# A complex state recurrence rewritten in a rotating frame, with the order of the convolution's taps changed

## The chip, the cores and the metric

One core of a Trainium2 chip runs the whole kernel. The metric is device microseconds (us) of one execution. Engines are named as in the profile: PE is TensorE (matmuls; PEld its weight loads), DVE VectorE, ACT ScalarE, POOL GpSimd, SP the engine that issues most DMAs.

## What is computed

Two layers of a hybrid block over 128 context tokens and 128 latent tokens (the two sequences are s = 0 and 1, NS = 2), width 1024, all in float32. One input projection feeds three branches: a convolution of width 31 over 512 channels, a bidirectional diagonal complex state space (S5, 32 groups of 16 channels, 64 complex states each) and attention with 8 query and 2 key heads. Gates, a merge and an output projection follow. The part of the reference that the change concerns:

```python
def _ssm_combine(e1, e2):
    a1, b1 = e1
    a2, b2 = e2
    return a1 * a2, a2 * b1 + b2
...
        lam_bar = jnp.exp(lam * dt)
        b_bar = ((lam_bar - 1.0) / lam)[..., None] * lax.complex(b_re[dirn], b_im[dirn])
        bu = jnp.einsum('blgc,gpc->blgp', uc, b_bar)
        if not want_final:
            bu = bu.at[:, edge].add(lam_bar * h0)
        a = jnp.broadcast_to(lam_bar, bu.shape)
        _, hs = lax.associative_scan(_ssm_combine, (a, bu), axis=1, reverse=rev)
        if want_final:
            fin = hs[:, 0] if rev else hs[:, -1]
        y = y + jnp.einsum('blgp,gcp->blgc', hs, c_mat).real
```

## The kernel before

Every engine runs one list of stages, written by hand in `order(l)` (one call for each layer), and does of each stage its own part, in the order of the list; semaphores join them. Weights come through SP as slabs of 512 KB into a ring of four (`raw`). For the early projections (`cg`, `ssm`, `ca`) and the late ones, ScalarE (L1086) and VectorE (L1358) split each weight chunk into a high and a low part and TensorE multiplies three times (L1032 to L1034); `q`, `kv`, `sg`, `gg` and `ag` are plain float32 (L756).

The state space works on chunks of L = 4 tokens, so 32 chunks (NCHUNK) and 32 steps. The partitions hold 64 forward and 64 backward states. The stages around the change, in the list's order:

- `tab` (L1466 on): VectorE and ScalarE make the powers of lambda and tables of them, from small parameters; GpSimd computes from them and B the matrices `pre` (`preP`), which TensorE transposes to E (`preE`). The tables of layer 1 are made in layer 0, after `att` 0.
- `xn`: ScalarE squares and sums x, GpSimd makes the rsqrt (L1783, L1779), VectorE scales x into `xn`, which lies in H (L1529). TensorE transposes it (`hT`).
- `pack`, `UT`: the tokens' inputs go through DMA and a ScalarE copy (L1229) into groups, TensorE transposes them, ScalarE and VectorE copy them to Uz (L1567).
- `S`: TensorE multiplies E by Uz (L867), eight banks; ScalarE copies the forward half to H, VectorE the backward half (L1575).
- `cp`: GpSimd computes CP, the powers times C (L1779, tiles tA, tB and EC), in 18 instructions, once the last bank of S is filled. `K` (TensorE, L880) needs CP, and the Toeplitz blocks M (`toeplitz`, 20 small DMAs) need K.
- `scan`: 32 steps of four VectorE instructions of 128 elements (`scan_step`, L1391). In steps 16 to 31 a tap of the convolution (`conv_tap`, L1423, 128x256) follows each; 31 taps for each of the tiles 0 and 1. The tiles 2 and 3 have their taps in `att` 1 and later.
- `qkn`: norms and rotary of q and k on VectorE, with a rsqrt on GpSimd, and a wait for it, for each sequence.
- `Y`: ScalarE and VectorE copy quarters of H to HY (L1296, L1676), TensorE multiplies (L961, L963), ScalarE copies out. Then `qkT` (transposes of q and k; VectorE copies to kz, L1630), `att` 0, and `gelu` (VectorE adds, ScalarE, L1312), whose result TensorE transposes in `geT` (L765) before `att` 1.

VectorE helpers: `tt_` is L1358, so that line has nearly all of its tensor_tensors; `needs` and `makes` put waits only on what an instruction reads.

```python
                    for c in range(c0, c1):
                        for i in range(4):
                            scan_step(l, c, i)
                            if taps_left:
                                conv_tap(*taps_left.pop(0))
```

## Time and profile before

| | |
|---|---|
| three runs | 846.63, 848.39, 848.56 us |
| median | 848.39 us |
| span of the profiled execution, from the first to the last instruction | 845.0 us |
| its own time | not given apart from the span |
| PE busy | 712.7 us, 84% |
| DVE busy | 605.8 us, 72% |
| ACT busy | 316.0 us, 37% |
| POOL busy | 172.6 us, 20% |
| mean granted TensorE clock | 0.936 |
| chain that ended last | PE 52%, DVE 36%, ACT 3%, DMA 3% |

A timeline row has start, duration, engine, line, operation, out<-in, shapes and count; in brackets stands the idle time of the engine before it and what ended it. Where a row counts several instructions, the duration is that of all. A row of a stretch has, after its length, the busy time and count of each engine, then the clock granted to TensorE as a share of full speed (1.00 is 2.4 GHz, its other level is 1.2 GHz), the DMA engines' share and GB/s. On the chain shares say who ended last, not what is slow: an engine may stand in it for work that another delayed.

### The profile page before, as it was taken

How to read it: one execution, taken by the hardware profiler on the slowest of the kernel's cores; microseconds unless marked ns; L12 is line 12 of the kernel's file. 1: busy time of each engine (PE TensorE's matmuls, PEld its weight loads, DVE VectorE, ACT ScalarE, POOL GpSimd, SP SyncE). 2: the span in 40 equal slices, each digit the busy share in tenths (PEclk: the TensorE clock that was granted, in tenths of full speed). 3: DMA queues.
4: the chain of work that ended last, by engine and by line, in shares of the span. 5: the costliest groups of instructions: out<-in, count | busy, mean ns of one | idle time of the engine just before them, and what ended most of it. 6: DMA issues, size and time to landing. Idle time of an engine off the chain costs nothing.

```text
span 845.0 us, 9392 instructions
## 1 busy us (share of the span) xinstructions
PE 712.7 (84%) x3294; PEld 469.8 (56%) x3294; DVE 605.8 (72%) x1103; ACT 316.0 (37%) x563; POOL 172.6 (20%) x121
## 2 busy tenths in 40 slices
PE   4957899990779994988999999999907698999996
PEld 1145665550721533776778558655507456787785
DVE  3378689997355589768866554899973568888664
ACT  1244451111323322454655355401213433545552
POOL 1067449202000009033000100492020000000000
PEclk9979999995789997999999999999967698999999
DMA  6864335350067471554565475454220034555661
GB/s 208 282 146 118 125 128 173 110 145 28 3 155 232 141 239 61 150 150 146 154 184 168 147 236 165 137 166 118 73 99 1 26 99 124 176 174 155 195 177 55
DMA packets 79339, 117.64 MB, mean 139 GB/s; under 512 B 27437, under 2 KB 31869, under 8 KB 79293
## 3 DMA queue, kind: packets, MB, share of 16 engines
q1 hardware_dynamic: 78460, 116.52, 45.6%
q10 hardware_dynamic: 832, 0.53, 0.3%
q8 instruction: 26, 0.43, 0.2%
q14 instruction: 21, 0.16, 0.1%
HBM read 112.51 MB, written 1.38 MB: 135 GB/s over the span
## 4 chain that ended last, share of the span: by engine, by line
PE 52%; DVE 36%; ACT 3%; DMA 3%; issue 2%; SPq 2%; POOL 1%; DVEq 0%; ACTq 0%; POOLq 0%
PE proj L1032 11%; PE proj L1034 10%; PE proj L1033 10%; DVE H L1358 8%; PE proj L730 8%; DVE cvacc L1423 7%; DVE qkt L1358 7%; PE side L765 4%; PE proj L756 3%; DVE qM_split L1358 3%; PE side L963 2%; DVE wide_split L1358 2%; DMA raw<-in_w_ada 2%; DVE H L1575 2%; DVE gates_split L1358 2%
## 5 line engine op out<-in xcount | busy, mean ns | idle before, releaser
L756 PE MATMUL proj<-raw,hT 128*128 128x512 f32 (+1 forms) x320 | 125.1, 551 | 0.0
L1423 DVE SCALAR_TENSOR_TENSOR cvacc<-cvpad,taps,cvacc 128x256 f32<-128x256 f32 x240 | 123.1, 541 | 0.0
L1358 DVE TENSOR_TENSOR wide_split<-raw,wide_split 128x512 fp32r<-128x512 f32 x118 | 90.6, 773 | 41.4 <-ACT wide_split L1086 40.3
L1086 ACT ACTIVATE wide_split<-raw 128x512 fp32r<-128x512 f32 x118 | 74.4, 632 | 95.9 <-PE proj L1034 95.9
L756 PEld LDWEIGHTS proj<-raw,hT 128*128 128x128 f32 x320 | 60.3, 190 | 60.4 <-issue 58.4
L730 PE MATMUL proj<-raw,cond 128*2 128x512 f32 x192 | 88.8, 617 | 5.9 <-DMA raw<-in_w_ada 5.9
L1358 DVE TENSOR_TENSOR H<-H,qkt 128x128 f32<-128x128 f32 x128 | 75.5, 590 | 1.2
L1032 PE MATMUL proj<-wide_split,H_split 128*128 128x512 f32 x154 | 65.0, 422 | 13.2 <-DVE wide_split L1358 12.7
L1783 POOL TENSOR_SCALAR st<-st 128x1 f32<-128x1 f32 (+1 forms) x12 | 3.9, 324 | 336.9 <-DVE st L1692 148.7
L961 PE MATMUL side<-qM,Uz 128*64 128x64 f32 x128 | 20.5, 248 | 54.3 <-DVE HY L1676 54.3
L1033 PE MATMUL proj<-wide_split,H_split 128*128 128x512 f32 x154 | 62.8, 408 | 0.0
L1034 PE MATMUL proj<-wide_split,H_split 128*128 128x512 f32 x154 | 62.7, 407 | 0.0
L1358 DVE TENSOR_TENSOR utok_split<-raw,utok_split 128x512 fp32r<-128x512 f32 x58 | 45.4, 783 | 16.9 <-ACT utok_split L1086 16.0
L730 PEld LDWEIGHTS proj<-raw,cond 128*2 128x2 f32 x192 | 15.6, 87 | 71.0 <-issue 56.1
L1358 DVE TENSOR_TENSOR qM_split<-raw,qM_split 128x512 fp32r<-128x512 f32 x32 | 38.6, 1218 | 20.3 <-ACT qM_split L1086 20.3
L1086 ACT ACTIVATE utok_split<-raw 128x512 fp32r<-128x512 f32 x58 | 36.6, 632 | 41.3 <-PE proj L1034 41.3
L961 PEld LDWEIGHTS side<-qM,Uz 128*64 128x64 f32 x128 | 15.0, 162 | 55.9 <-issue 55.9
L1032 PEld LDWEIGHTS proj<-wide_split,H_split 128*128 128x128 f32 x154 | 29.9, 194 | 26.4 <-DVE wide_split L1358 18.6
L1032 PE MATMUL proj<-qM_split,mixed_split 128*128 128x512 f32 x64 | 27.4, 428 | 13.6 <-DVE qM_split L1358 13.6
L1358 DVE TENSOR_TENSOR qkt<-H,lamI 128x128 f32<-128x128 f32 x64 | 37.3, 583 | 1.4
L1196 ACT ACTIVATE gates<-proj 128x512 f32<-128x512 f32 x12 | 7.1, 597 | 75.9 <-PE proj L756 62.6
L1779 POOL TENSOR_TENSOR tA<-cT,lamr 128x1024 f32<-128x1024 f32 (+1 forms) x12 | 19.7, 1640 | 74.5 <-PE side L867 73.7
(235 smaller groups left out, 1491.1 us busy)
## 6 DMA issues: line engine op xcount, KB each, us to landing
raw<-in_w_in SPq DMA_DIRECT2D x104, 512.0 KB, 3.8
raw<-in_w_ada SPq DMA_DIRECT2D x48, 512.0 KB, 4.5
raw<-in_w_out SPq DMA_DIRECT2D x16, 512.0 KB, 4.2
raw<-in_w_ssm_glu SPq DMA_DIRECT2D x8, 512.0 KB, 5.2
raw<-in_w_ssm_out SPq DMA_DIRECT2D x8, 512.0 KB, 3.8
raw<-in_w_attn_out SPq DMA_DIRECT2D x8, 512.0 KB, 4.1
raw<-in_w_conv_out SPq DMA_DIRECT2D x8, 512.0 KB, 3.9
raw<-in_w_in SPq DMA_DIRECT2D x8, 256.0 KB, 2.8
```

Of the source, the lines that this page charges most:

```text
L730: m = T.matmul(proj.bank(stg + (b,))[0:NS, :], cond[:, :, kt], w[:, 0, W * b:W * b + W], start=(kt == 0), stop=(kt == DT - 1))
L756: m = T.matmul(proj.bank((l, u, s))[:, 0:n], lhs[:, s, kt, :], w[:, i, :], start=(kt == 0), stop=last)
L765: return T.transpose(out, in_, ident[0:k, 0:k])
L961: T.matmul(o, Uz[:, g, :], M[:, :, g // 2, :], start=True, stop=False)
L963: m = T.matmul(o, HY[:, q % 2, gi, r, :, :].rearrange("p s k -> p (s k)"), CP[:, r, 1:L + 1, g, :], start=False, stop=(r == 1))
L1032: T.matmul(bank[:, :], hi, whi, start=(kt == 0), stop=False)
L1033: T.matmul(bank[:, :], hi, wlo, start=False, stop=False)
L1034: m = T.matmul(bank[:, :], lo, whi, start=False, stop=last)
L1086: S.activation(chunk_parts(m)[0], chunk_raw(m), ACT.Copy).then_inc(chunk_hi, 1)
L1358: return V.tensor_tensor(out, a, b, op)
L1423: m = V.scalar_tensor_tensor(acc, src, taps[:, t, j:j + 1], acc, ALU.mult, ALU.add)
L1779: return Q.tensor_tensor(out, a, b, op)
```

## The change

The recurrence h(k+1) = lambda h(k) + b(k), with complex lambda, is written for h turned back by the angle of lambda times k. There the factor is the real decay, the same for real and imaginary part, and a quarter of the groups (8 of 32; 1024 elements in a lane) is done by one scan instruction (tensor_tensor_scan, listed as SCALAR_TENSOR_TENSOR of H from decay and H). VectorE turns b by a table `spin` of cosines and sines, scans, and turns back in place; Y reads H directly, so HY's copies go. GpSimd makes `spin` by doubling (5 rounds of 4 instructions) from lambda's angle. H has a new layout, with the chunks innermost. ScalarE now copies both halves of S. The taps of tiles 0 and 1 stand in three blocks of 14, 24 and 24: before `UT`, behind `qkn`, and behind `tab` and `spin` (in layer 1 behind `att` 0). `convT` moves ahead of `pack`. The tables lamR, lamI and the tile h0 go; the scratch for DMA rings is smaller, and the semaphores follow.

```diff
 def order(l):
...
-            + [("unit", "ssm"), ("unit", "ca"), ("pack",)] + ([("preE", 0, 1)] if l == 0 else [])
-            + [("bz", 0), ("UT",), ("S",), ("cp",), ("convT", 0), ("convT", 1), ("scan", 0, 16, ()),
-               ("unit", "q"), ("unit", "kv"), ("scan", 16, NCHUNK, (0, 1)),
-               ("unit", "sg"), ("K", 0), ("bz", 1), ("qkn", 0), ("qkn", 1)]
+            + [("unit", "ssm"), ("unit", "ca"), ("convT", 0), ("convT", 1), ("pack",)]
+            + ([("preE", 0, 1)] if l == 0 else [])
+            + [("bz", 0), ("conv", 0, 7, (0, 1), None), ("UT",), ("S",), ("cp",), ("unit", "q"), ("unit", "kv")]
+            + [("states", i) for i in range(4)]
+            + [("unit", "sg"), ("K", 0), ("bz", 1), ("qkn", 0), ("qkn", 1), ("conv", 7, 19, (0, 1), None)]
             + [("unit", "gg"), ("K", 1), ("unit", "ag"), ("Y",), ("qkT", 0), ("qkT", 1), ("att", 0)]
-            + nxt("small", n) + nxt("tab", n) + nxt("ada", n, 0) + nxt("adaT", n, 0)
+            + nxt("small", n) + nxt("tab", n) + nxt("spin", n) + [("conv", 19, TAPS, (0, 1), None)]
+            + nxt("ada", n, 0) + nxt("adaT", n, 0)
...
 def stages():
-    out = [(0, s) for s in (("cond",), ("small", 0), ("tab", 0), ("taps", 0), ("ada", 0, 0), ("xn", 0, 0), ("xn", 0, 1),
+    out = [(0, s) for s in (("cond",), ("small", 0), ("tab", 0), ("spin", 0), ("taps", 0), ("ada", 0, 0), ("xn", 0, 0), ("xn", 0, 1),
...
-        H, Hs = shared("H", [P, NCHUNK + 1, ROW])
+        H, Hs = shared("H", [P, G, 2, NS, NCHUNK])
...
 TensorE, stage Y
-                        pe.wait_ge(hy_fwd, 4 * l + q + 1)
-                        pe.wait_ge(hy_bwd, 4 * l + q + 1)
+                        pe.wait_ge(states_done, 4 * l + q + 1)
...
-                                m = T.matmul(o, HY[:, q % 2, gi, r, :, :].rearrange("p s k -> p (s k)"),
+                                m = T.matmul(o, H[:, g, r, :, :].rearrange("p s k -> p (s k)"),
...
 ScalarE, stage S
-                        dst = H[0:64, 1:NCHUNK + 1, 16 * i:16 * i + 16].rearrange("p k x -> p x k")
-                        S.activation(dst, side.bank(key)[0:64, :].rearrange("p (x k) -> p x k", k=NCHUNK),
-                                     ACT.Copy).then_inc(side.freed(key), 1)
+                        src = side.bank(key)[:, :].rearrange("p (x k) -> p x k", k=NCHUNK)
+                        dst = H[:, 4 * i:4 * i + 4, :, :, :].rearrange("p g r s k -> p (g r s) k")
+                        S.activation(dst[0:64], src[0:64], ACT.Copy).then_inc(side.freed(key), 1)
+                        S.activation(dst[64:128, :, ::-1], src[64:128], ACT.Copy).then_inc(side.freed(key), 1)
...
 VectorE
-            def scan_step(l, c, i):
...
+            def states(l, q):
+                g0 = GQ * q
+                here = H[:, g0:g0 + GQ, :, :, :]
+                lanes = lambda t: t.rearrange("p g r s k -> p g (r s) k")
+                for i in (2 * q, 2 * q + 1):
+                    side.drained(dve, ("S", l, i))
+                if q == 0:
+                    side.filled(dve, ("E", l, 7))
+                    dve.wait_ge(zeroed, N_ZERO)
+                    dve.wait_ge(tab_done, l + 1)
+                    dve.wait_ge(spin_done, l + 1)
+                def turn(k0):
+                    for i in range(2):
+                        by = spin[:, i, g0:g0 + GQ, k0:k0 + NCHUNK].unsqueeze(2).to_broadcast([P, GQ, 2 * NS, NCHUNK])
+                        makes(("turned", i), tt_(lanes(turned[i]), lanes(here), by))
+                if q:
+                    dve.wait_ge(states_done, 4 * l + q)
+                turn(1)
+                makes("decay", V.tensor_copy(decay[:, :, :, 1:NCHUNK], ss[:, 14, g0:g0 + GQ].unsqueeze(2).unsqueeze(3)
+                                             .to_broadcast([P, GQ, 2 * NS, NCHUNK - 1])))
+                needs(("turned", 0), ("turned", 1))
+                for r, op in ((0, ALU.add), (1, ALU.subtract)):
+                    tt_(here[:, :, r, :, 1:NCHUNK], turned[0][:, :, r, :, 0:NCHUNK - 1],
+                        turned[1][:, :, 1 - r, :, 0:NCHUNK - 1], op)
+                    tt_(ends[:, 0, r, g0:g0 + GQ], turned[0][:, :, r, 0, NCHUNK - 1], turned[1][:, :, 1 - r, 0, NCHUNK - 1], op)
+                V.memset(here[:, :, :, 0, 0], 0.0)
+                makes("here", V.tensor_copy(here[:, :, :, 1, 0], t5[:, 3:5, g0:g0 + GQ].rearrange("p r g -> p g r")))
+                needs("here", "decay")
+                flat = here.rearrange("p g r s k -> p (g r s k)")
+                makes("here", V.tensor_tensor_scan(flat, decay[:, :, :, :].rearrange("p g x k -> p (g x k)"), flat, 0.0,
+                                                   ALU.mult, ALU.add))
+                needs("here")
...
+                turn(0)
...
+                needs(("turned", 0), ("turned", 1))
+                for half in range(2):
+                    rows_ = slice(64 * half, 64 * half + 64)
+                    for r, op in ((0, ALU.subtract), (1, ALU.add)):
+                        dst = here[rows_, :, r, :, :]
+                        if half:
+                            dst = dst[:, :, :, ::-1]
+                        m = tt_(dst, turned[0][rows_, :, r, :, :], turned[1][rows_, :, 1 - r, :, :], op)
+                m.then_inc(states_done, 1)
...
 GpSimd
+                elif k == "spin":
+                    ll = stg[1]
+                    pool.wait_ge(tab_done, ll + 1)
+                    for w in (1, 2, 4, 8, 16):
+                        n = 2 * G * w
+                        t1, t2 = (t[:, 0:n].rearrange("p (r g k) -> p r g k", r=2, g=G) for t in (tB, bzf))
+                        known = spin[:, :, :, 1:w + 1]
+                        by = [spin[:, r:r + 1, :, w:w + 1].to_broadcast([P, 2, G, w]) for r in range(2)]
+                        link(tt_(t1, known, by[0]))
+                        link(tt_(t2, known, by[1]))
+                        link(tt_(spin[:, 0, :, w + 1:2 * w + 1], t1[:, 0], t2[:, 1], ALU.subtract))
+                        m = tt_(spin[:, 1, :, w + 1:2 * w + 1], t1[:, 1], t2[:, 0], ALU.add)
...
```

How the instructions stand, at three places. First VectorE in layer 0, from the end of the early projections to the recurrence; `mixed` is the convolution's input, Uz the state space's input by groups. Before:

```order
L1546 SCALAR_TENSOR_TENSOR mixed<-th,proj 128x512 x2
L1567 COPY Uz<-side 64x8x64 x2
L1575 COPY H<-side 64x16x32 x8
L1583 COPY H<-h 128x128
L1358 TENSOR_TENSOR qkt<-H,lamI 128x128
L1358 TENSOR_TENSOR qkt<-H,lamR 128x128
L1358 TENSOR_TENSOR H<-H,qkt 128x128 x2
```

And with the change, behind the same row of `mixed`:

```order
L1452 TENSOR_SCALAR cvacc<-cvpad,taps 128x256 x2
L1455 SCALAR_TENSOR_TENSOR cvacc<-cvpad,taps,cvacc 128x256 x12
L1596 COPY Uz<-side 64x8x64 x2
L1351 TENSOR_TENSOR pre<-H,spin 128x1024 x2
L1405 COPY decay<-ss 128x32x31
L1351 TENSOR_TENSOR H<-pre 128x8x2x31
L1351 TENSOR_TENSOR ends<-pre 128x8
L1351 TENSOR_TENSOR H<-pre 128x8x2x31
L1351 TENSOR_TENSOR ends<-pre 128x8
L1412 MEMSET H 128x16
L1413 COPY H<-t 128x16
L1416 SCALAR_TENSOR_TENSOR H<-decay,H 128x1024
```

Fourteen taps (cvacc) now stand ahead of Uz, and in place of eight copies and the first of 32 steps the rows show the first half of one quarter of four.

Second GpSimd at the start, from the spread of the time steps to the rsqrt of x (the rows with st). Before:

```order
L1790 MEMSET st 128x12
L1796 COPY a<-ldt 32x128
L1783 ISA
L1783 TENSOR_SCALAR st<-st 128x1
L1779 TENSOR_TENSOR st<-st 128x1
```

And with the change, from the third round of the doubling on:

```order
L1776 TENSOR_TENSOR tB<-spin 128x256
L1776 TENSOR_TENSOR bz<-spin 128x256
L1776 TENSOR_TENSOR spin<-tB,bz 128x32x4 x2
L1776 TENSOR_TENSOR tB<-spin 128x512
L1776 TENSOR_TENSOR bz<-spin 128x512
L1776 TENSOR_TENSOR spin<-tB,bz 128x32x8 x2
L1776 TENSOR_TENSOR tB<-spin 128x1024
L1776 TENSOR_TENSOR bz<-spin 128x1024
L1776 TENSOR_TENSOR spin<-tB,bz 128x32x16 x2
L1780 TENSOR_SCALAR st<-st 128x1
L1776 TENSOR_TENSOR st<-st 128x1
```

The first two rounds, on 128x64 and 128x128, stand ahead of these. The rsqrt, the last two rows, now comes behind twenty instructions on `spin`.

Third VectorE in layer 0 behind `att` 0, from the end of `tab` for layer 1 to the bias and skip of Y (`utok`, `mixed`), whose sum the GELU takes. Before:

```order
L1515 COPY lamR<-lamr 128x128
L1519 TENSOR_SCALAR lamI<-lami 128x32x2
L1520 COPY lamI<-lami 128x32x2
L1522 MEMSET h 128x128
L1524 COPY h<-t 128x32
L1525 COPY h<-t 128x32
L1358 TENSOR_TENSOR ada<-side,modc 128x16
L1358 TENSOR_TENSOR utok<-utok,rows 128x512
L1358 TENSOR_TENSOR mixed<-mixed,utok 128x512
L1358 TENSOR_TENSOR utok<-utok,rows 128x512
L1358 TENSOR_TENSOR mixed<-mixed,utok 128x512
L1358 TENSOR_TENSOR ada<-side,modc 128x16
```

And with the change:

```order
L1351 TENSOR_TENSOR ss<-ss 128x32 x2
L1547 COPY ss<-tB 128x32
L1351 TENSOR_TENSOR ss<-bz 128x32 x2
L1351 TENSOR_TENSOR ss<-ss 128x32
L1552 TENSOR_SCALAR ss<-ss 128x32
L1351 TENSOR_TENSOR spin<-bz,ss 128x32 x2
L1455 SCALAR_TENSOR_TENSOR cvacc<-cvpad,taps,cvacc 128x256 x24
L1351 TENSOR_TENSOR ada<-side,modc 128x16
L1351 TENSOR_TENSOR utok<-utok,rows 128x512
L1351 TENSOR_TENSOR mixed<-mixed,utok 128x512
L1351 TENSOR_TENSOR utok<-utok,rows 128x512
L1351 TENSOR_TENSOR mixed<-mixed,utok 128x512
```

24 taps now stand between the table and the sum that the GELU waits for.

## Rows read from the trace of the kernel before

**Rows 1.** Busy time by stretch; the first line names the columns.
```profile
core 0: us, PE busy (x) PEld busy (x) DVE busy (x) ACT busy (x) POOL busy (x), PEclk, DMA share, GB/s
117.20:151.70 34.50, 34.50 (x99) 18.09 (x97) 33.93 (x30) 5.18 (x11) 31.66 (x18) 1.00 0.45 138
188.70:215.90 27.20, 0.03 (x2) 0.04 (x1) 21.95 (x54) 4.78 (x4) 4.36 (x4) 0.60 0.09 27
612.00:639.10 27.10, 0.00 (x0) 0.00 (x0) 21.85 (x54) 4.37 (x3) 4.36 (x4) 0.60 0.24 79
```

**Rows 2.** Timeline of PE: S and K in layer 0, geT, S in layer 1.
```profile
109.02 7.38 PE L867 MATMUL side<-Uz,EC 128*128 128x128 f32 x64 [1.01 <-DVE Uz L1567]
...
151.68 4.63 PE L880 MATMUL side<-EC,bz 128*48 128x80 f32 x64
...
275.55 1.09 PE L765 MATMUL side<-ident,mixed 128*128 128x128 f32 x8
...
532.29 7.38 PE L867 MATMUL side<-Uz,EC 128*128 128x128 f32 x64 [1.02 <-DVE Uz L1567]
```

**Rows 3.** Timeline of DVE and ACT: from qkn to the GELU, layer 0, then layer 1.
```profile
200.00 0.82 DVE L1358 TENSOR_TENSOR qkt<-qk 128x640 f32<-128x640 f32 x1
...
214.72 1.97 DVE L1676 COPY HY<-H 64x1024 f32<-64x1024 f32 x2
...
230.75 0.29 DVE L1630 COPY kz<-side 64x128 f32<-64x128 f32 x1 [5.57 <-PE side L765]
...
267.02 0.63 ACT L1312 ACTIVATE mixed<-mixed 128x512 f32<-128x512 f32 x1 [5.20 <-DVE mixed L1358]
...
654.00 0.29 DVE L1630 COPY kz<-side 64x128 f32<-64x128 f32 x1 [5.56 <-PE side L765]
...
668.29 0.63 ACT L1312 ACTIVATE mixed<-mixed 128x512 f32<-128x512 f32 x1 [3.61 <-DVE mixed L1358]
```

**Rows 4.** Timeline of DVE, one step alone, and of POOL in cp.
```profile
152.81 0.29 DVE L1358 TENSOR_TENSOR qkt<-H,lamI 128x128 f32<-128x128 f32 x1
...
153.87 0.29 DVE L1358 TENSOR_TENSOR qkt<-H,lamI 128x128 f32<-128x128 f32 x1
...
116.49 1.93 POOL L1779 TENSOR_TENSOR tA<-cT,lamr 128x1024 f32<-128x1024 f32 x1 [21.20 <-PE side L867]
...
120.52 2.47 POOL L1779 TENSOR_TENSOR EC<-tA,tB 128x1024 f32<-128x1024 f32 x1
...
148.80 1.39 POOL L1779 TENSOR_TENSOR EC<-tA,tB 128x512 f32<-128x512 f32 x1
```

**Rows 5.** Timeline of POOL and DVE in preP, layer 0.
```profile
86.57 2.36 POOL L1779 TENSOR_TENSOR tB<-lami,bbar 128x1024 f32<-128x1024 f32 x1
...
86.97 2.52 DVE L1358 TENSOR_TENSOR gates_split<-raw,gates_split 128x512 fp32r<-128x512 f32 x1
```

**Rows 6.** Timeline of DVE and ACT just before S, layer 0.
```profile
104.44 1.38 DVE L1546 SCALAR_TENSOR_TENSOR mixed<-th,proj 128x512 f32<-128x512 f32 x2 [2.06 <-PE proj L1034]
...
107.62 1.30 DVE L1567 COPY Uz<-side 64x512 f32<-64x512 f32 x2 [1.80 <-PE side L765]
...
101.56 1.90 ACT L1229 ACTIVATE HY<-wide 64x2048 f32<-64x2048 f32 x1
...
107.61 1.07 ACT L1237 ACTIVATE Uz<-side 64x512 f32<-64x512 f32 x2
```

**Rows 7.** Timeline of DVE with no POOL beside it: wide passes and taps.
```profile
304.93 2.36 DVE L1358 TENSOR_TENSOR H_split<-hT,H_split 128x1024 fp32r<-128x1024 f32 x2
307.21 8.80 DVE L1423 SCALAR_TENSOR_TENSOR cvacc<-cvpad,taps,cvacc 128x256 f32<-128x256 f32 x22
```

**Rows 8.** Timeline of POOL, DVE and PE at the start, around xn.
```profile
30.13 0.24 POOL L1783 TENSOR_SCALAR st<-st 128x1 f32<-128x1 f32 x1 [18.88 <-ACT H L1145]
...
32.33 0.75 DVE L1529 TENSOR_SCALAR H<-x,st 128x1024 f32<-128x1024 f32 x1 [0.43 <-POOL st L1779]
...
45.98 1.62 PE L765 MATMUL side<-ident,H 128*128 128x128 f32 x12
```

More of the change, by code:

```diff
@@ L62 @@
 GP = G // 2
-ROW = G * 2 * NS
+GQ = G // 4
 EPS = 1e-6
@@ L290, in build @@
         tt += [bzf[:, 352 * i:352 * i + 352] for i in range(4)]
-        lamR = sb("lamR", [P, ROW])
-        lamI = sb("lamI", [P, ROW])
+        spin = sb("spin", [P, 2, G, NCHUNK + 1])
+        ends = sb("ends", [P, 3, 2, G])
         a32 = sb("a32", [P, 5, P])
@@ L349, in build @@
         nmx = sb("nmx", [P, NS, HEADS, 2])
-        scan_t = qkt[:, 0:2 * ROW].rearrange("p (a b) -> p a b", a=2)
+        decay = sb("decay", [P, GQ, 2 * NS, NCHUNK])
+        turned = [pre[:, i, :, :, :].rearrange("p g j c -> p (g j c)").rearrange("p (g r s k) -> p g r s k", g=GQ, r=2, s=NS)
+                  for i in range(2)]
         ldt = sb("ldt", [P, 2])
@@ L468, in build @@
         ln_pre = sem("ln_pre")
-        N_ZERO = 4
+        N_ZERO = 7
         tab_dt = sem("tab_dt")
@@ L967, in _ @@
                     side.claim(pe, key)
+                    pe.wait_ge(ends_done, l + 1)
                     for r in range(2):
-                        src = H[:, NCHUNK, :].rearrange("p (g r s) -> p r s g", g=G, r=2)[:, r, 0, :]
-                        m = transpose(side.bank(key)[0:G, P * r:P * r + P], src)
+                        m = transpose(side.bank(key)[0:G, P * r:P * r + P], ends[:, 0, r, :])
                     m.then_inc(side.full, 1)
@@ L1631, in _ @@
                 elif k == "conv":
-                    end = 0 if stg[3] is None else chunk_at[(l, "br" + stg[3], WT - 1)] + 1
+                    end = 0 if stg[4] is None else chunk_at[(l, "br" + stg[4], WT - 1)] + 1
+                    if stg[1] == 0:
+                        conv_ready(l)
                     for j in range(stg[1], stg[2]):
-                        for t in (2, 3):
+                        for t in stg[3]:
                             conv_tap(t, j)
@@ L1789, in _ @@
             Q.memset(kz[1][:, :, :], 0.0).then_inc(zeroed, 1)
+            Q.memset(decay[:, :, :, 0], 0.0).then_inc(zeroed, 1)
+            Q.memset(spin[:, 0, :, 0], 1.0).then_inc(zeroed, 1)
+            Q.memset(spin[:, 1, :, 0], 0.0).then_inc(zeroed, 1)
             link(Q.memset(st[:, 128:140], -0.5))
@@ L1797, in _ @@
                                   ldt[0:G, :].unsqueeze(2).to_broadcast([G, 2, SP])).then_inc(ldt_spread, 1)
+                elif k == "spin":
[10 more added lines that the diff above has]
+                        m = tt_(spin[:, 1, :, w + 1:2 * w + 1], t1[:, 1], t2[:, 0], ALU.add)
+                        if w < 16:
+                            link(m)
+                        else:
+                            m.then_inc(spin_done, 1)
+                            pool.wait_ge(spin_done, ll + 1)
                 elif k == "preP":
```

136 lines of the change are left out of this document (43 added, 93 removed).

## The prediction, made before the changed kernel had run

> **What bounds the kernel now.** I read the busy time by stretch first [rows 1]. TensorE works in nearly all of the stretch from 117 to 152 us. From 188.7 to 215.9 us it does almost nothing (0.03 of 27.2 us), and in layer 1 from 612.0 to 639.1 us nothing (27.1 us). VectorE has 22 us of work in each. So twice 27 us is the most that a shorter recurrence could give at these places.
>
> The timelines say what the wait is made of. Call S the start of the matmuls that fill the recurrence's input, 109.02 us in layer 0 and 532.29 in layer 1 [rows 2]; I count from it. VectorE copies, scans 32 steps, normalises q and k from 200.00 to 214.72 (14.7 us, with two waits for GpSimd), and only then makes the copies that Y needs [rows 3]. The first copy of kz, with which attention starts, comes at 230.75, that is S + 121.7; in layer 1 at 654.00, again S + 121.7.
>
> The scan is not long because of its own instructions. A step that runs alone takes 153.87 - 152.81 = 1.06 us. But from 116.49 to 150.19 GpSimd computes CP in 18 tensor_tensor instructions [rows 4], and in the 34.5 us of [rows 1] VectorE gets only 30 instructions through, between seven and eight steps: about 26 us are lost. With wider instructions the exchange is the same: GpSimd's 128x1024 instruction in [rows 5] takes 2.36 us where it takes 1.93 beside short ones [rows 4], and VectorE's 128x512 subtraction takes 2.52 where one of that width takes 0.69 alone (1.38 for two, [rows 6]). One of VectorE's passes gets in for each of GpSimd's, and their times add up.
>
> **The recurrence, costed.** A quarter has two rotations of two 128x1024 products, the decay table, two pairs of an add with 496 elements and a tiny one, small fills, the scan instruction, and four 64x512 adds. Two 128x1024 passes take 2.36 us [rows 7], about 1.14 from start to start. So: rotations 4 x 1.14 = 4.6. Decay 0.6 (a 128x1024 single-input instruction took 0.75 [rows 8]; a 1x copy would be 1.1). 496- and 512-wide adds at half of the 1024's price and a little overhead, 6 x 0.6 = 3.6. Small ones and their waits 0.9. The scan instruction is in no row. Its lower end is one 128x1024 pass, 1.2 us. Its upper end is a quarter of today's steps, 32 x 1.06 / 4 = 8.5 us. I take 1.2, since the operand shapes are those of that pass. Sum 10.9 a quarter, 43.6 a layer. That replaces 32 steps (some 30 us of own time with taps laid between them), copies of S (7 us) and of HY (4 us): no saving in own time.
>
> The Trainium skill (DVE: opcode table, instruction layouts, handler registers and perf-mode slots, section Datapath and trigger behaviour) says that the built-in tensor_tensor_scan runs at half throughput; by it the scan would cost about 1.2 us more a quarter, and that is a rival below. No run here shows it.
>
> GpSimd's CP work, 150.19 - 116.49 = 33.7 us [rows 4], now falls wholly on that chain: its 18 instructions meet 18 of VectorE's, long ones, and where 26 us were lost before, 33.7 are. GpSimd is held up in turn by about 8 us.
>
> **The chain from S to kz.** First two banks drained by ScalarE, each in two copies of 0.53 us (two such took 1.07, [rows 6]): 3.3. Quarters 43.6. CP 33.7. Final states 0.6. Normalisation 14.7. Then 24 taps, which the new order puts ahead of kz: 22 take 8.80 us [rows 7], so 9.6. Sum S + 105.5 instead of S + 121.7: 16.2 us earlier in each layer. TensorE would allow a little more. CP ends at about S + 7.5 + 33.7 + 8 = S + 49.5 where K is wanted at 151.68, S + 42.7 [rows 2], a new wait of 7 us; with the rest of the units and the transfers of the Toeplitz blocks Y starts near S + 89, takes 11, and kz could come at S + 102. It is hidden behind VectorE by 3 us.
>
> **What the reordering costs before S.** VectorE's last product ends at 105.8 and it copied Uz at 107.62 [rows 6]. Now TensorE transposes the convolution's input, ScalarE copies it (to 107.1) and packs only then (1.90 us), and VectorE does 14 taps (5.5 us) before Uz. Uz starts at about 112.6, S at 114.0: 5.0 us later in layer 0, 5.2 in layer 1. VectorE was idle here for 2 us, so only these are free.
>
> **The spin table on GpSimd.** 20 instructions in five doublings, 5952 elements per lane. From 2.47 us for 1024 and 1.39 for 512 [rows 4] an instruction costs 0.31 us and 2.1 ns an element, 1.6 where an operand is broadcast, plus 0.08 between two: 18 us. Its lower bound is the elements at 1.6 ns with nothing else, 10 us; its upper one every element at 2.1 ns, 20 us. In layer 0 it stands ahead of the two rsqrt, which now run from 30.13 [rows 8]. They move to about 49.5, the two xn behind them end at 52.2, then come two small drains and a transpose, and the transposes of H that started at 45.98 start at about 53: 7 us later, with nothing to cover them, since the first projections wait for hT.
>
> In layer 1's table (made in layer 0, after attention) VectorE has 24 taps just behind the table. Each waits for one of GpSimd's 20: 18 + 20 x 0.17 + 4 x 0.4 = 22.6 us, of which 9.6 are the taps' own. The bias add and GELU stand behind them.
>
> **The sum.** Layer 0: S comes at 109.0 + 7 + 5 = 121.0. From kz to the GELU takes 267.02 - 230.75 = 36.3 us now [rows 3] and 36.3 + 22.6 = 58.9 then. GELU at S + 105.5 + 58.9 = 285.4, the transposes of it 0.7 later, at 286.1. They start now at 275.55 [rows 2], set by TensorE and the ada weights, with 8 us of slack to the GELU. That slack goes first; the loss is 10.6, and 2 more for TensorE, which sits idle for some 15 us and starts att(1) at the lower of its two clock levels, 1.2 GHz of 2.4 (after each idle stretch of [rows 1], where the granted clock is 0.60, the next work starts so). So +13, and nothing between 300 and 478 us can take it back, as that stretch is not changed. Layer 1: S +5.2, kz -16.2, then 24 taps ahead of the GELU (668.29, 14.3 us behind kz [rows 3]) +9.6: -1. Together +12 us. The page gives only the span, 845.0 us, 3.4 below the median of the runs shown, 848.4; I put the difference on the median: **860 us**, slower. A table of 14 us instead of 18 counts twice and gives 852; one of 20 and a decay table at 1.1 us in 8 quarters give 868: this case reaches from 852 to 868.
>
> **Rivals.**
> - *The scan instruction costs two passes.* 2.36 us for two 128x1024 passes [rows 7], 1.2 us more in each of 8 quarters, all on the chain that binds in both layers: 9 us more, 869 us. For it: each element needs the one before. Against it: no row. Chance 0.28. Near the upper end of 8.5 us, that is, if the one instruction does not do what it is said to, it would be 58 us more; 0.03.
> - *Faster: GpSimd's CP no longer costs VectorE its whole time.* If a long VectorE instruction runs on beside it, as [rows 5] denies for 512 elements but no row shows for 1024, the chain loses 10 us instead of 33.7, and TensorE binds. Kz comes at S + 102 in both layers. Layer 0: S at 121.0, kz at 223.0, GELU 36.3 + 9.6 behind it (the taps run beside the table), its transposes at 269.6, -6. Layer 1: 5.2 - 19.7 + 9.6 = -5. 837 us. It decides from the point at which 12 us of the chain go, counting both layers. Against it speaks that every wide instruction in [rows 5] is held. The Trainium skill (SBUF — State Buffer, section SBUF: two separate sides) speaks against it too: the pair of ports is locked for a whole instruction; the 2.52 us agrees with it. Chance 0.20, which takes in waits whose order I have wrong.
> - *The spin table is short*, near 10 us: 8 less before hT and up to 8 less behind the table, 848 us, no change. Chance 0.09.
>
> **How the numbers follow.** Forecast 0.40, half-rate scan 0.28, upper end 0.03, faster 0.20, short table 0.09. Within 0.3% (2.5 us, about what a measurement of this kernel can tell from no change) lies half of the short table, 0.05. Faster is 0.20 and a third of the short table, 0.23; slower is the rest, 0.72. The range runs from the faster case's centre, 838, to 874 above the half-rate scan: it leaves out half of the faster case, the upper end and a tail.
>
> **What would show it.** GpSimd: 20 short instructions ahead of the first rsqrt, which starts near 49 us. VectorE: the quarters end 81 us behind S, tensor_tensors of 3 us during CP, taps of 0.9 us and more beside the spin table. TensorE: idle 5 us before S, 7 us before K, 10 to 17 us before the GELU's transposes, but only a few before Y. I am wrong if the quarters end within 70 us of S, or if TensorE has no idle time before the GELU's transposes in layer 0.

## The result, and the profile after

The changed kernel takes 863.38 us (median of 4 runs, 862.64 to 865.4) beside 847.51 us of the kernel before (4 runs, 846.03 to 848.56). The ratio is 1.0203, with a 95% interval of 1.0177 to 1.0229: it is slower by 16 to 17 us. The profiled execution took 863.71 us, its span is 861.9 us.

The page of the changed kernel: the head of its part 1, then the same engines' digits and TensorE's granted clock in 40 slices.

```profile
PE 722.9 (84%) x3294; PEld 476.9 (55%) x3294; DVE 630.0 (73%) x975; ACT 306.2 (36%) x571; POOL 230.7 (27%) x164
...
PE   4928779779877697698999999698698398999996
...
PEclk9968989979989699799999999899799598999999
```

TensorE's waits, longest sums first (what waited, what it waited for; us in total, times, the longest).

```profile
PE side L767 <- ACT mixed L1305: 26.7, 4, 13.4
PE side L883 <- POOL EC L1776: 20.8, 2, 10.6
PE proj L1034 <- DVE wide_split L1351: 12.9, 9, 4.5
PE proj L1034 <- DVE qM_split L1351: 12.7, 7, 8.3
PE side L869 <- DVE Uz L1596: 6.9, 2, 4.0
```

The 27 us before Y in each layer [rows 1] are gone. In their place stand 13 us before the GELU's transposes and 10 us before K, twice each, and smaller waits before S and before the first projections.

TensorE's timeline gives the places that answer to [rows 2] (start, length, what, how many; in brackets the idle time ahead and what ended it): the transposes of H, S, K, Y and the GELU's transposes of layer 0, then S and K of layer 1.

```profile
52.34 3.77 PE L767 MATMUL side<-ident,H 128*128 128x128 f32 x16
...
122.17 10.44 PE L869 MATMUL side<-Uz,EC 128*128 128x128 f32 x64 [2.90 <-DVE Uz L1596]
...
177.12 7.42 PE L883 MATMUL side<-EC,bz 128*48 128x80 f32 x64 [10.13 <-POOL EC L1776]
...
218.81 0.33 PE L963 MATMUL side<-qM,Uz 128*64 128x64 f32 x2 [1.85 <-DMA qM<-wide]
...
288.05 1.12 PE L767 MATMUL side<-ident,mixed 128*128 128x128 f32 x4 [12.93 <-ACT mixed L1305]
...
555.58 9.54 PE L869 MATMUL side<-Uz,EC 128*128 128x128 f32 x64 [3.96 <-DVE Uz L1596]
...
610.14 6.00 PE L883 MATMUL side<-EC,bz 128*48 128x80 f32 x64 [10.65 <-POOL EC L1776]
```

With these and the same places of the kernel before, the time can be followed through the span (us; a shift is after minus before, the forecast's is summed up from its terms):

| place | before | after | shift | forecast |
|---|---|---|---|---|
| transposes of H, layer 0 | 45.98 | 52.34 | +6.4 | +7 |
| S, layer 0 | 109.02 | 122.17 | +13.2 | +12 |
| first copy of kz, layer 0 | 230.75 | 231.26 | +0.5 | -4.2 |
| GELU's transposes, layer 0 | 275.55 | 288.05 | +12.5 | +10.6 |
| the ada matmuls behind att(1) | 299.95 | 316.23 | +16.3 | +12.6 |
| S, layer 1 | 532.29 | 555.58 | +23.3 | +17.8 |
| first copy of kz, layer 1 | 654.00 | 662.01 | +8.0 | +1.6 |
| GELU's transposes, layer 1 | 668.97 | 686.35 | +17.4 | +11.2 |
| end | 845.0 | 861.9 | +16.9 | +11.2, given as 12 |

The stretch from S to kz did become shorter, by 12.6 us in layer 0 and 15.3 in layer 1. That is not the recurrence's own gain: 38 of the 62 taps left this stretch too, some 15 us of VectorE's time at 0.40 us a tap, and they come back ahead of S and ahead of the GELU. The rest of the change takes more than the stretch gives.

VectorE's timeline, for the quarters. The first four lines belong to quarter 1 and lie beside CP, which GpSimd began at 132.70 us (the quarter itself began at 127.26); the next seven are most of quarter 4, with no CP beside it; the last two are the two groups of 24 taps in layer 0, the first alone and the second beside the spin table.

```profile
134.00 1.72 DVE L1351 TENSOR_TENSOR ends<-H,ss 128x16 f32<-128x16 f32 x1
135.65 4.09 DVE L1351 TENSOR_TENSOR pre<-H,spin 128x1024 f32<-128x1024 f32 x2
139.66 2.31 DVE L1351 TENSOR_TENSOR ends<-ends 128x16 f32<-128x16 f32 x1
141.90 8.12 DVE L1351 TENSOR_TENSOR H<-pre 64x512 f32<-64x512 f32 x4
...
191.32 2.36 DVE L1351 TENSOR_TENSOR pre<-H,spin 128x1024 f32<-128x1024 f32 x2
193.60 0.67 DVE L1405 COPY decay<-ss 128x992 f32<-128x992 f32 x1
...
195.75 2.29 DVE L1416 TENSOR_TENSOR_SCAN H<-decay,H 128x1024 f32<-128x1024 f32 x1
198.07 0.18 DVE L1351 TENSOR_TENSOR ends<-H,ss 128x16 f32<-128x16 f32 x1
198.17 2.35 DVE L1351 TENSOR_TENSOR pre<-H,spin 128x1024 f32<-128x1024 f32 x2
200.44 0.17 DVE L1351 TENSOR_TENSOR ends<-ends 128x16 f32<-128x16 f32 x1
200.55 2.60 DVE L1351 TENSOR_TENSOR H<-pre 64x512 f32<-64x512 f32 x4
...
218.60 9.60 DVE L1455 SCALAR_TENSOR_TENSOR cvacc<-cvpad,taps,cvacc 128x256 f32<-128x256 f32 x24
...
266.12 19.80 DVE L1455 SCALAR_TENSOR_TENSOR cvacc<-cvpad,taps,cvacc 128x256 f32<-128x256 f32 x24
```

A quarter alone takes 203.15 - 191.32 = 11.8 us (the last add ends at 203.15), and the scan instruction (here listed as TENSOR_TENSOR_SCAN) 2.29 of them. Beside CP the four adds of 64x512 take 8.12 us instead of 2.60, and an instruction of 16 elements a lane takes 2.31 instead of 0.17. What an instruction pays there does not follow its length: the scan in quarter 2 takes 3.11 us, 0.8 more than alone, and one add of 496 elements there takes 0.66, no more than alone.

### The profile page after: what moved, and what is told of

Its sections match the earlier page's. It is cut to its first block and busy times, and to the rows that moved or that the text cites. A ratio compares the mean times of both kernels' runs of the same rounds, so it can differ in the third digit from the quotient of the medians.

```text
span 861.9 us, 9320 instructions
## 1 busy us (share of the span) xinstructions
PE 722.9 (84%) x3294; PEld 476.9 (55%) x3294; DVE 630.0 (73%) x975; ACT 306.2 (36%) x571; POOL 230.7 (27%) x164
## 5 line engine op out<-in xcount | busy, mean ns | idle before, releaser
L1455 DVE SCALAR_TENSOR_TENSOR cvacc<-cvpad,taps,cvacc 128x256 f32<-128x256 f32 x240 | 118.8, 562 | 0.1
L1351 DVE TENSOR_TENSOR pre<-H,spin 128x1024 f32<-128x1024 f32 x32 | 50.6, 1622 | 10.8 <-issue 10.0
L1351 DVE TENSOR_TENSOR qM_split<-raw,qM_split 128x512 fp32r<-128x512 f32 x32 | 36.0, 1136 | 21.5 <-ACT qM_split L1088 21.5
L1776 POOL TENSOR_TENSOR tA<-cT,lamr 128x1024 f32<-128x1024 f32 (+1 forms) x12 | 26.2, 2183 | 91.7 <-PE side L869 90.9
L1351 DVE TENSOR_TENSOR H<-pre 64x512 f32<-64x512 f32 (+1 forms) x48 | 49.5, 1056 | 0.1
L1034 PEld LDWEIGHTS proj<-wide_split,H_split 128*128 128x128 f32 x154 | 29.9, 194 | 26.0 <-DVE wide_split L1351 18.7
L883 PE MATMUL side<-EC,bz 128*48 128x80 f32 x256 | 22.7, 260 | 20.8 <-POOL EC L1776 20.8
L883 PEld LDWEIGHTS side<-EC,bz 128*48 128x48 f32 x256 | 22.0, 143 | 24.0 <-POOL EC L1776 22.4
L1036 PEld LDWEIGHTS proj<-wide_split,H_split 128*128 128x128 f32 x154 | 30.2, 196 | 7.3
```

Of the source, the lines that this page charges most:

```text
L883: m = T.matmul(side.bank(key)[0:48, 80 * b:80 * b + 80], bz[:, r, g % 16, :], CP[:, r, :, g, :], start=(r == 0), stop=(r == 1))
L1034: T.matmul(bank[:, :], hi, whi, start=(kt == 0), stop=False)
L1036: m = T.matmul(bank[:, :], lo, whi, start=False, stop=last)
L1351: return V.tensor_tensor(out, a, b, op)
L1455: m = V.scalar_tensor_tensor(acc, src, taps[:, t, j:j + 1], acc, ALU.mult, ALU.add)
L1776: return Q.tensor_tensor(out, a, b, op)
```

## The experiments

My theory was that four separate costs lie on one chain (the spin table ahead of the rsqrt, the same table beside the taps, CP beside the quarters, the later S) and that the recurrence gains 10 to 16 us a layer against them. The rivals were that one or the other cost is hidden anyway, or that VectorE's time is long for a reason of its own. All runs were made beside runs of the kernel before, whose median moved between 844.65 and 847.51 us; so the ratio to those is compared, and a gain given in us is a difference of two ratios times 845 us. The changed kernel has 1.0203.

| run | us, median | before beside it | ratio, 95% interval | span |
|---|---|---|---|---|
| e1_spin0_late | 854.35 | 844.65 | 1.0114 (1.0078 to 1.015) | 851.2 |
| e2_spin1_late | 863.45 | 844.65 | 1.0223 (1.0187 to 1.0259) | 860.6 |
| e3_cp_vector | 843.47 | 844.65 | 0.9986 (0.9965 to 1.0007) | 843.7 |
| e5_taps_behind_s | 855.48 | 844.65 | 1.0125 (1.0098 to 1.0153) | 853.3 |
| e4_before_cp_vector | 829.58 | 845.54 | 0.9816 (0.9749 to 0.9884) | 827.8 |
| e7_spin1_waits | 852.59 | 845.54 | 1.0104 (1.007 to 1.0138) | 850.7 |
| e8_product_for_scan | 839.2 | 845.54 | 0.9933 (0.9909 to 0.9958) | 837.1 |
| e6_four_edits | 821.16 | 845.54 | 0.9718 (0.9666 to 0.977) | 820.2 |
| e9_taps_in_gaps | 817.39 | 845.85 | 0.9654 (0.9637 to 0.9671) | 815.9 |
| e10_before_taps_in_gaps | 810.91 | 845.85 | 0.9574 (0.9555 to 0.9594) | 806.9 |
| e11_spin1_behind_cback | 808.05 | 846.73 | 0.9558 (0.952 to 0.9595) | 806.1 |

### The spin table ahead of the first rsqrt

```
-  ("tab", 0), ("spin", 0), ("taps", 0), ("ada", 0, 0), ("xn", 0, 0), ("xn", 0, 1),
+  ("tab", 0), ("taps", 0), ("ada", 0, 0), ("xn", 0, 0), ("xn", 0, 1), ("spin", 0),
```

> The spin table of layer 0 stands behind the two rsqrt instead of ahead of them on GpSimd. Theory (the table's place costs its whole length at the start): the transposes of H go back from 52.3 to about 46 us, the first projection from 64.4 to about 57, S from 122.2 to about 114.5; nothing later takes it back, so about 7 us less than the changed kernel, near 856. Rival (the table only moves to another cover): GpSimd's next work, the convolution of B with its table, starts at 52.7 us now and would start no earlier, so the E transposes and S hold at 120 or later; less than 3 us gained, 861.

The transposes of H start at 45.22 us, the first projection at 55.96 and S at 113.38. The time is 0.9% lower, 7.5 us. The table's place costs its delay whole. Behind the two rsqrt it holds up nothing at the start: the transposes of H stood at 45.98 us before the change.

### The spin table beside the taps: one miss, then the answer

e2_spin1_late moves the stage of layer 1's table behind the GELU's transposes in the list:

```
-  nxt("tab", n) + nxt("spin", n) + [("conv", 19, TAPS, (0, 1), None)]
+  nxt("tab", n) + [("conv", 19, TAPS, (0, 1), None)]
...
-  [("geT", 0), ("geT", 1)] + nxt("adaT", n, 1)
+  [("geT", 0), ("geT", 1)] + nxt("adaT", n, 1) + nxt("spin", n)
```

> Layer 1's spin table is made behind the GELU's stage, beside the second attention, instead of ahead of the 24 taps. Theory (the 24 taps run at half speed only because of it): the taps take 9.6 us instead of 19.8, the GELU's transposes start near 278 instead of 288.05, TensorE waits about 3 us there instead of 12.9; about 10 us less, 853, or 12 less if the second attention also starts at the higher clock. Rival: the table then meets VectorE's work of the second attention, which TensorE waits for after every score, and holds it up by as much; the ada work behind it starts no earlier than 313 (316.2 now) and the time is 859 or more.

Neither theory was tried by it: GpSimd's first instruction of the table began at 266.01 us and the taps took 19.79 us, as without the edit. A stage's place in the list orders an engine's own work only, and GpSimd had nothing between. e7_spin1_waits adds what holds it:

```
                     pool.wait_ge(tab_done, ll + 1)
+                    if ll:
+                        pool.wait_ge(gelu_pre, NS * ll)
```

> As e2_spin1_late, with a wait on GpSimd for the bias adds of the GELU, since its place in the list alone did not hold the table back: GpSimd had nothing else to do and began at 266.01 us as before. Theory: the 24 taps take 9.6 us instead of 19.8, the GELU's transposes start near 278 instead of 288, about 10 us less than the changed kernel: a ratio to before of 1.008 to 1.011. Rival: the table meets VectorE in the second attention and the loss only moves there: 1.016 or more.

Timelines of e7_spin1_waits: VectorE's 24 taps, GpSimd's first instruction of the table, and TensorE's GELU transposes.

```profile
264.18 9.58 DVE L1455 SCALAR_TENSOR_TENSOR cvacc<-cvpad,taps,cvacc 128x256 f32<-128x256 f32 x24
...
276.64 0.35 POOL L1776 TENSOR_TENSOR tB<-spin 128x64 f32<-128x64 f32 x1 [37.97 <-DVE mixed L1351]
...
275.89 1.11 PE L767 MATMUL side<-ident,mixed 128*128 128x128 f32 x4 [3.30 <-ACT mixed L1305]
```

The taps are back at 9.58 us, TensorE's wait falls from 12.93 to 3.30 us, and the ratio from 1.0203 to 1.0104: 8 us. The second attention, where VectorE's taps now meet the table, takes no more than in the changed kernel: from the GELU's transposes to the ada matmuls (303.64 us) it is 27.75 us, there 28.18. But it does not come back to the 24.40 us of the kernel before.

### CP beside the quarters

e3_cp_vector removes CP's 18 instructions from GpSimd and issues the same ones on VectorE, behind the first quarter:

```
-  ("S",), ("cp",), ("unit", "q"), ("unit", "kv")] + [("states", i) for i in range(4)]
+  ("S",), ("unit", "q"), ("unit", "kv")] + [("states", 0), ("cp",)] + [("states", i) for i in range(1, 4)]
```

> CP is computed by VectorE itself, between the first and the second quarter, not by GpSimd beside them. Theory (the quarters are stretched by GpSimd's instructions and by nothing else): every quarter takes 11.9 us; CP's 12 passes of 128x1024 at 1.14 us and 6 of 128x512 at 0.6 are 17.3 us, 18 with their waits; VectorE's chain from the first to the last quarter is 4 x 11.9 + 18 = 66 instead of 75.9, TensorE's wait of 10.1 us before K is gone, kz comes some 10 us earlier in each layer: 20 less, 843. Rival (the stretch belongs to the drains of S or to the wide instructions themselves, whatever GpSimd does): the quarters stay at 75.9 and 18 come on top in each layer, 885 or more. Second rival (TensorE or the transfers of the Toeplitz blocks bind from there on): quarters as in the theory, but kz only 3 to 6 us earlier a layer, 850 to 856.

Timeline of VectorE in e3_cp_vector: the first instruction of CP, its last, and the second quarter's first and last group.

```profile
138.66 1.23 DVE L1351 TENSOR_TENSOR tA<-cT,lamr 128x1024 f32<-128x1024 f32 x1
...
156.66 0.69 DVE L1351 TENSOR_TENSOR EC<-tA,tB 128x512 f32<-128x512 f32 x1
157.27 2.35 DVE L1351 TENSOR_TENSOR pre<-H,spin 128x1024 f32<-128x1024 f32 x2
...
166.49 2.59 DVE L1351 TENSOR_TENSOR H<-pre 64x512 f32<-64x512 f32 x4
```

CP takes 18.6 us of VectorE in each layer, where GpSimd beside it had cost it 28.5 (75.9 us for the four quarters less 4 x 11.85), and the second quarter takes 11.8 us instead of the 28.2 it took beside CP (150.15 to 178.35). TensorE no longer waits before K. The ratio falls from 1.0203 to 0.9986, 18 us, as forecast: 18.6 us more work a layer for VectorE made the kernel faster. The same edit on the kernel before:

> The kernel before, with CP computed by VectorE ahead of the old 32-step recurrence. Theory (it is GpSimd's instructions that stretch VectorE's, whatever the recurrence): about 26 us were lost beside CP, CP itself takes VectorE 18.6 us as measured in the run before, so VectorE's chain is 7 to 8 us shorter in each layer; in layer 1 that shows whole, in layer 0 the GELU's transposes are held by the ada weights and little shows: 8 to 15 us less than before, a ratio of 0.982 to 0.991. Rival (what helped the changed kernel was TensorE's wait before K, 10.1 us there, which does not exist before): no gain, a ratio of 1.00 or above. It also says what the changed recurrence itself is worth once neither kernel has GpSimd beside it.

It gives 0.9816, 16 us, with TensorE's wait before Y at 19.3 us in each layer instead of 27.2. So the loss is one of GpSimd beside VectorE, and the kernel before pays it too: the same edit is worth 16 us there and 18 here, which the intervals can't tell apart. CP is the largest of the four costs in the changed kernel, but hardly a part of what made it slower than the kernel before: with CP on VectorE in both, 0.9986 stands against 0.9816, 14 of the 17 us. The others, the table's two places and the order ahead of S, make up the difference, less what the stretch from S to kz gives back. That layer 0 gained as much as layer 1 I had not expected: the GELU's transposes moved from 275.55 to 265.75, and the wait for the ada weights ahead of them is 5.0 us long as before: the whole place, that wait with it, moved 9.8 us, so layer 0 has no fixed bound there.

### The taps ahead of S

```
-  ("unit", "ca"), ("convT", 0), ("convT", 1), ("pack",)]
+  ("unit", "ca"), ("pack",)]
...
-  [("bz", 0), ("conv", 0, 7, (0, 1), None), ("UT",), ("S",), ("cp",), ("unit", "q"), ("unit", "kv")]
+  [("bz", 0), ("UT",), ("S",), ("cp",), ("convT", 0), ("convT", 1), ("unit", "q"), ("unit", "kv")]
...
-  ("qkn", 1), ("conv", 7, 19, (0, 1), None)]
+  ("qkn", 1), ("conv", 0, 19, (0, 1), None)]
```

> The transposes of the convolution's input and its first 14 taps go back behind S; the taps stand with the 24 behind the normalisation of q and k. Theory (VectorE and TensorE bind almost alike before kz: VectorE is ready 3.1 us ahead of kz in layer 0 and 0.8 us in layer 1): S is 5 us earlier in both layers, kz 5.6 later behind the normalisation, less the 3.1 and 0.8: 2.6 us gained in layer 0, none in layer 1: 860 to 861. Rival (TensorE binds alone and the taps are hidden): 10 us less, 853. Rival (the taps ahead of S cost nothing, since S is not on the path): 863 to 868.

It gives 1.0125, 6.6 us, between the expected 2.6 and the rival's 10. About 2 us of the trace are not the edit's: the first projection starts at 62.30 instead of 64.40, ahead of everything that the edit moves (why is not shown). For the rest, S came 7.1 us earlier behind the GELU of layer 0 (260.4 instead of 267.5 us from those transposes to S) where I had expected 5, and kz stands 110.1 us behind S in both layers instead of 109.1 and 106.4. The terms had the right signs, but my price of the order ahead of S was too low.

### What the scan instruction costs

e8_product_for_scan is e3_cp_vector with

```
-  V.tensor_tensor_scan(flat, decay..., flat, 0.0, ALU.mult, ALU.add)
+  tt_(flat, decay..., flat, ALU.mult)
```

> e3_cp_vector with the eight scan instructions replaced by a plain product of the same operands: the recurrence along the chunks is left out, and the final states and Y are not the reference's. Theory (a scan costs two passes, 2.29 us against 1.2 of a product): the product takes 1.2 us, VectorE's chain to kz is 4.4 us shorter in each layer, of which TensorE lets 3.3 through (Y ends at 215.99, kz at 219.32): 6 to 8 us less than e3_cp_vector, a ratio to before of 0.990 to 0.992. Rival (the 2.29 us belong to the operands, which are read and written in the same place, and not to the scan): the product takes 2.3 us too and the time does not move, 0.998.

The kernel of this run leaves out the sum along the chunks, so it serves for the time alone.

The instructions of e8_product_for_scan that write or read H, two of the groups (count; ns least/median/most, first and last start).

```profile
L1351 DVE TENSOR_TENSOR pre<-H,spin x32: 1208/1218/1226, 126.7 to 606.6; 128x1024 f32<-128x1024 f32 x32
...
L1351 DVE TENSOR_TENSOR H<-decay,H x8: 1224/1226/1586, 131.1 to 604.1; 128x1024 f32<-128x1024 f32 x8
```

The same operands, read and written in the same place, take 1.23 us as a product and 2.29 us as a scan, and the ratio falls from 0.9986 to 0.9933, 4.5 us. VectorE was 1.06 us shorter in each of eight quarters, 8.5 us; about half of that reached the end, as TensorE was ready only 3.3 us ahead of kz in layer 0. The rule of the Trainium skill (DVE: opcode table, instruction layouts, handler registers and perf-mode slots, section Datapath and trigger behaviour), that the built-in scan runs at half throughput, agrees with these two times, whose ratio is 1.9.

### The costs together

e6_four_edits has the edits of e1, e7, e3 and e5 together.

> The changed kernel with four edits together: layer 0's spin table behind the rsqrt, layer 1's behind the GELU's adds, CP on VectorE between the first and second quarter, the 14 taps behind S. Theory (the costs lie at different places of one chain and add up): 7.5 + 10 + 18.5 + 1 to 3 = 37 to 39 us less than the changed kernel, some 823 to 825, a ratio to before of 0.975 to 0.978. Rival (once VectorE is faster TensorE and the ada weights bind, and the savings overlap): a ratio of 0.983 or more.

0.9718: 41 us less than the changed kernel, where the single edits gave 7.5, 8, 18 and 6.6, 40 in sum, and 37 to 39 were expected. The costs lie one behind the other.

### What the recurrence itself is worth

With the taps free of the recurrence they can go where VectorE waits. In e9_taps_in_gaps the loop of att(0) gets 20 of them, and 24 go behind the GELU's adds (layer 0) or among the chunks of branch B (layer 1):

```
                         if s == 1:
                             for j in (2 * p, 2 * p + 1):
                                 for t in (2, 3):
                                     conv_tap(t, j)
+                        else:
+                            for j in (9 + 2 * p, 10 + 2 * p):
+                                for t in (0, 1):
+                                    conv_tap(t, j)
```

> e6_four_edits with the first tiles' taps put where VectorE waits: 18 of the 38 stay ahead of kz, 20 go between the steps of the first attention, the last 24 behind the GELU's adds in layer 0 and among the chunks of the branch B in layer 1. Theory (VectorE binds before kz and ahead of the GELU; taps in its gaps cost nothing): kz comes 6 us earlier in each layer, where TensorE then binds (Y ended at 203.8, kz at 210.0); the GELU's transposes 3 us more in layer 0 and 9.6 us more in layer 1. 20 to 24 less than e6_four_edits, a ratio to before of 0.943 to 0.949, 797 to 802. Rival (the attentions and chunk stages have no gaps that long, and each tap delays a step that TensorE waits for): a ratio of 0.962 or more.

It gave 0.9654, 5 us where I had expected over 20, and the trace names two reasons. From e9_taps_in_gaps: VectorE's 24 taps behind the GELU's adds, TensorE in the second attention, and what TensorE waited for from 640 us on (us in total, times, the longest).

```profile
244.69 19.81 DVE L1455 SCALAR_TENSOR_TENSOR cvacc<-cvpad,taps,cvacc 128x256 f32<-128x256 f32 x24
...
268.13 1.08 PE L767 MATMUL side<-ident,pre 128*128 128x128 f32 x4 [10.46 <-ACT pre L1287]
...
PE proj L1034 <- DVE wide_split L1351: 4.4, 9, 0.6
...
PE proj L1034 <- DVE utok_split L1351: 2.8, 5, 0.7
```

I had moved the taps to the one place at which the spin table was now released. The second reason is that the 24 taps of layer 1 are not free among the chunks of branch B: from the GELU's transposes to the end it takes 183.4 us (632.47 to 815.9), where e6_four_edits takes 175.9 (644.27 to 820.2), and the two waits above are 0.7 and 1.2 us there. The other moves did what they should, or most of it: kz at S + 97.8 instead of S + 101.6 in layer 0 and S + 95.4 instead of S + 101.3 in layer 1, where 6 us less had been expected, and the GELU's transposes of layer 1 at 18.2 us behind the transposes of q instead of 32.5. The same moves of taps on the kernel before, with its 32 steps, and CP on VectorE as in e4_before_cp_vector:

```
-  taps_left = [(t, j) for t in tiles for j in range(TAPS)]
+  taps_left = [(t, j) for t in tiles for j in range(9)]
```

> The kernel before with its old 32-step recurrence, CP on VectorE, and 44 of the 62 taps taken out of the recurrence and put in the same gaps as in e9_taps_in_gaps. It tells what the new recurrence itself is worth. Theory (from S to kz VectorE needs the same time with either recurrence once the taps are counted: 112.0 us in e4_before_cp_vector with 62 taps inside, 97.3 in e3_cp_vector with 24, and 38 taps at 0.4 us are 15.2): taking 44 taps out shortens the old chain by up to 17.6 us a layer, so this kernel ends within 6 us of e9_taps_in_gaps, a ratio to before of 0.943 to 0.957. Rival (the old recurrence's steps leave bubbles in which the taps were free, and only the new form gains by moving them): a ratio of 0.975 or more, hardly below e4_before_cp_vector.

0.9574, 20 us less than e4_before_cp_vector: the old recurrence is faster than e9_taps_in_gaps. The last run moves the table on to a place where TensorE alone is busy:

```
-  ("cback", 0), ("cback", 1), ("comb", "C", 1)]
+  ("cback", 0), ("cback", 1)] + nxt("spin", n) + [("comb", "C", 1)]
```

> e9_taps_in_gaps, with layer 1's spin table moved on behind the second rsqrt of the convolution's normalisation, where GpSimd rests from 394 to 469 us and TensorE is never kept waiting. Theory (what kept e9_taps_in_gaps above its forecast is this table once more: released by the GELU's adds it ran beside the 24 taps, which took 19.81 us, and TensorE waited 10.46 us in the second attention): the taps take 9.6 us, that wait goes, 10 to 12 us less, 805 to 808, a ratio to before of 0.951 to 0.955, that is no better than e10_before_taps_in_gaps with its old recurrence by more than 6 us. Rival (the table holds up VectorE's subtractions in the chunk stage instead, which TensorE then waits for): a ratio of 0.960 or more.

In e11_spin1_behind_cback the taps take 9.58 us and the second attention starts without that wait. The ratio is 0.9558 (0.952 to 0.9595), that of the old recurrence 0.9574 (0.9555 to 0.9594): these runs can't tell the two apart. In the traces the new form has kz 2.0 us (layer 0) and 2.5 us (layer 1) earlier behind S (S + 96.1 and 95.6, against 98.1 in both), but it takes 3.0 us longer from kz of layer 0 to S of layer 1 (304.3 against 301.2; why is not shown), and the spans are 806.1 and 806.9 us. The 7.5 us behind the GELU of layer 1 stay in both (183.4 us to the end in each). Both kernels are some 4.3% faster than the kernel before and 6% faster than the changed one, and nothing of it that these runs can show, to some 4 us, comes from the rotating frame.

VectorE's timeline says the same. From S to the normalisation of q and k, with CP on VectorE in both, e3_cp_vector needs 194.97 - 122.01 = 73.0 us without a single tap. e10_before_taps_in_gaps needs 177.17 - 108.76 = 68.4 us with 18 taps (7.2 us) inside; its copies of HY come later, 4.1 us. Timeline of VectorE there: a step alone, the first instruction of the normalisation, and the first group of HY's copies.

```profile
176.11 0.29 DVE L1358 TENSOR_TENSOR qkt<-H,lamI 128x128 f32<-128x128 f32 x1
176.32 0.28 DVE L1358 TENSOR_TENSOR qkt<-H,lamR 128x128 f32<-128x128 f32 x1
176.53 0.61 DVE L1358 TENSOR_TENSOR H<-H,qkt 128x128 f32<-128x128 f32 x2
177.17 0.82 DVE L1358 TENSOR_TENSOR qkt<-qk 128x640 f32<-128x640 f32 x1
...
191.90 1.97 DVE L1703 COPY HY<-H 64x1024 f32<-64x1024 f32 x2
```

So the new form holds VectorE 8 us longer in layer 0 (73.0 against 61.2 + 4.1); 4.9 of the 73.0 are VectorE's wait for ScalarE's copies of S, of which it made half itself before. What the new form has for that is that Y reads H itself and no longer waits for copies behind the normalisation, and that the taps are free; the second can be had without it.

## Why the prediction was right

The forecast was 860 us, 11.6 above the median shown; measured are 863.38, 15.9 above the median beside it. Sign, size and range (838 to 874) hold, and the mechanism forecast is by and large the one that the trace shows: CP's cost lies on the chain, the table stands ahead of the rsqrt and beside the taps. The step from the old kernel to the new one, though, is not CP: by the forecast its cost rose from 26 to 33.7 us a layer, and by e3_cp_vector and e4_before_cp_vector it hardly rose. That the sum came out within 5 us owes something to errors of both signs. The terms one by one:

- **A quarter** was put at 10.9 us and takes 11.8. The scan was the miss: I took 1.2 and it takes 2.29, as the rival said to which I gave 0.28. It cost 8.5 us of VectorE's time, and by e8_product_for_scan half of that in the end.
- **CP** was put at 33.7 us on the chain and cost 75.9 - 4 x 11.85 = 28.5, about 1 of it from GpSimd's copies for bz beside quarter 3 (12.97 us). The two errors cancel, with a third (the first quarter starts 5.1 us behind S, not 3.3), and I must call that luck: the quarters end 81.0 us behind S (203.15) in layer 0, as stated, and 80.6 in layer 1.
- **K** was to wait 7 us and waits 10.1 and 10.7. I let CP start 7.5 us behind S and last 33.7 + 8 (which ends at S + 49.2 and not at the 49.5 that I wrote). It starts 10.5 behind and lasts 44.4. The start is late since the 64 matmuls of S take 10.44 us and not 7.38 [rows 2]. About 1.1 us of that come with the new division of the copies: in e5_taps_behind_s and e6_four_edits, at a granted clock of 1.00, the same matmuls take 8.53 us, and in e6_four_edits TensorE waits 0.8 us for ScalarE, which now makes both halves of the copies. The rest goes with the clock: it is 0.67 in the first 9.38 us of them, where it was 1.00 before, and ahead of them TensorE had waited 1.61 us and 2.90 us, where it had waited 1.01. K itself takes 7.42 and 6.00 us, where it took 4.63 [rows 2]. With that TensorE, and not VectorE, sets kz in layer 0, S + 109.1 instead of S + 105.5; VectorE was ready 3.1 us earlier. In layer 1 it is S + 106.4.
- **The order ahead of S** was put at 5.0 and 5.2 us. It is 7 in layer 1 (S shifts from 16.4, where the first transposes of layer 1 stand, to 23.3). TensorE waits 2.48 us for the pack and 3.96 for Uz there; I counted one of the two. Over both layers that is 3.6 us too little, as much as the late kz of layer 0.
- **The spin table** was put at 18 us; it takes 16.8 at the start and 18.1 in layer 0's second half. The transposes of H came 6.4 us later (7 forecast), the 24 taps beside it take 19.80 us (22.6 forecast; the terms as written add up to 23.0).
- **TensorE's clock**: I put 2 us for the second attention, and it is 3.8: from the GELU's transposes to the ada matmuls it takes 24.40 us before and 28.18 after.

Busy time by stretch over S in layer 0, and then over the second attention, of the changed kernel, and last over S in layer 0 of e6_four_edits (the columns are named in [rows 1]). PEclk is 0.67 and 0.87 in the first two; the kernel before has 1.00 in both, so a part of each stretch ran at 1.2 GHz and not at 2.4.

```profile
122.17:131.55 9.38, 9.38 (x57) 9.33 (x57) 4.29 (x9) 6.05 (x11) 0.00 (x0) 0.67 0.01 2
...
288.05:316.23 28.18, 27.97 (x104) 16.02 (x104) 14.13 (x34) 10.78 (x26) 0.00 (x0) 0.87 0.23 65
...
108.42:116.95 8.53, 8.29 (x64) 7.50 (x64) 4.79 (x10) 7.09 (x12) 0.00 (x0) 1.00 0.28 103
```

The rival of a gain (CP not at VectorE's whole cost) fell: it needed 10 us of loss in place of 33.7, and 28.5 were measured. The short table fell with 16.8 and 18.1 us. Both signs that I had named as fatal stayed away: the quarters do not end within 70 us of S, and TensorE waits 12.93 us before the GELU's transposes, inside the 10 to 17 that I gave.
